# Attention with the value product turned round, logits as three products of split halves, and a ring of four heads

## What is computed

```python
logits = jnp.einsum('btkgd,btskd->btkgs', qg, k_sel).astype(f32) * ATT_SCALE
logits = jnp.where(valid[:, :, None, None, :], logits, -jnp.inf)
probs = jax.nn.softmax(logits, axis=-1).astype(v.dtype)
o = jnp.einsum('btkgs,btskd->btkgd', probs, v_sel)
return (o.reshape(B, L, ATT_WIDTH) * jax.nn.silu(z)) @ w_out
```

## Time and profile before

| | us |
|---|---|
| median of 3 runs | 1507.84 |
| lowest and highest | 1505.77, 1508.29 |
| the profiled execution | 1508.62 |
| its span | 1506.8 |
| busy in it: TensorE products, weight loads | 1404.7, 1220.5 |
| busy in it: VectorE, ScalarE, GpSimd | 933.7, 643.4, 559.2 |

### The profile page before, as it was taken

The page is one execution under the profiler, slowest core; times in us unless marked ns, Lnnn a source line. Parts: engine busy times, 40 slices in busy tenths (PEclk is TensorE's granted clock), DMA queues, the critical chain, the costliest instruction groups (busy, mean ns, idle before and its releaser), DMA issues. The chain is left out here.

```text
span 1506.8 us, 21428 instructions
## 1 busy us (share of the span) xinstructions
PE 1404.7 (93%) x8109; PEld 1220.5 (81%) x8109; DVE 933.7 (62%) x1765; ACT 643.4 (43%) x1136; POOL 559.2 (37%) x402
## 2 busy tenths in 40 slices
PE   4999999999996899999988999999999999998898
PEld 3999746999995455548878998989999999997786
DVE  7111388787793989744556676667676757576333
ACT  6233464677664555541122625243434343443121
POOL 4276501265553001100012646465555556464000
PEclk9999999999998999999998999999999999999899
DMA  6112100232312410001231101010101111105221
GB/s 223 29 43 57 28 1 15 72 87 75 96 48 67 140 29 15 4 24 63 100 88 43 43 20 57 20 57 20 57 27 50 35 43 34 43 6 201 99 85 63
DMA packets 96181, 86.79 MB, mean 58 GB/s; under 512 B 4528, under 2 KB 84272, under 8 KB 96080
## 3 DMA queue, kind: packets, MB, share of 16 engines
q1 hardware_dynamic: 94448, 80.60, 17.3%
q0 software_dynamic: 1632, 4.82, 0.9%
HBM read 65.43 MB, written 19.97 MB: 57 GB/s over the span
## 5 line engine op out<-in xcount | busy, mean ns | idle before, releaser
L186 PE MATMUL bank<-hn_hi,rw_hi 128*128 128x352 f32 x768 | 250.8, 327 | 1.5 <-PEq L1059 1.5
L186 PE MATMUL bank<-hn_hi,rw_lo 128*128 128x352 f32 x768 | 247.6, 322 | 0.0
L186 PE MATMUL bank<-hn_lo,rw_hi 128*128 128x352 f32 x768 | 247.3, 322 | 0.0
L186 PE MATMUL bank<-hn_hi,w_hi 128*128 128x352 f32 x672 | 218.9, 326 | 3.6 <-PEq L274 3.6
L186 PE MATMUL bank<-hn_lo,w_hi 128*128 128x352 f32 x672 | 216.4, 322 | 0.0
L186 PE MATMUL bank<-hn_hi,w_lo 128*128 128x352 f32 x672 | 216.2, 322 | 0.0
L186 PEld LDWEIGHTS bank<-hn_hi,rw_hi 128*128 128x128 f32 x768 | 144.9, 189 | 3.4 <-issue 3.0
L186 PEld LDWEIGHTS bank<-hn_lo,rw_hi 128*128 128x128 f32 x768 | 145.3, 189 | 0.0
L186 PEld LDWEIGHTS bank<-hn_hi,rw_lo 128*128 128x128 f32 x768 | 144.9, 189 | 0.0
L186 PEld LDWEIGHTS bank<-hn_hi,w_hi 128*128 128x128 f32 x672 | 126.9, 189 | 4.3 <-issue 3.7
L186 PEld LDWEIGHTS bank<-hn_lo,w_hi 128*128 128x128 f32 x672 | 127.2, 189 | 0.0
(11 more groups left out here) (233 smaller groups left out, 2950.5 us busy)
## 6 DMA issues: line engine op xcount, KB each, us to landing
rw_raw<-in_rec_w_in SPq DMA_DIRECT2D x32, 512.0 KB, 4.0
w_raw<-in_att_w_in SPq DMA_DIRECT2D x30, 512.0 KB, 4.0
q_rotated<-relu SPq DMA_DIRECT2D x24, 176.0 KB, 1.9
xin<-in_x_prompt SPq DMA_DIRECT2D x8, 512.0 KB, 4.1
q_tile<-q_rotated SPq DMA_DIRECT2D x8, 512.0 KB, 3.7
wo_raw<-in_att_w_out SPq DMA_DIRECT2D x4, 1024.0 KB, 10.0
x_again<-in_x_prompt SPq DMA_DIRECT2D x8, 512.0 KB, 4.1
residual<-h_rows SPq DMA_DIRECT2D x8, 512.0 KB, 2.9
```

The source lines that it names most:

```text
L186: last = pe.matmul(out, l, r, start=n == 0, stop=n == len(passes) - 1)
```

## The change

- **Value product.** It is made for each head. The transposed probabilities of a key tile are the loaded operand, and the 128 columns of a value head stream, so the output stands as queries by head width. It comes two items behind the transposes, at step i for item i-6. `pT` becomes a ring of four heads (`P_SLOTS`), freed head by head.
- **Sums.** The probabilities are no longer divided. Once for four heads VectorE takes the reciprocals (`divide`) and multiplies the output of the value product out of PSUM into `o_rows` (`scale`). TensorE turns each head back with a transpose into the same PSUM bank (`turn`), and the gate follows. The transposes of the probabilities wait for the exponential.
- **Logits** of tiles 2 to 7 (`FINE`): three float32r products of split halves in place of the plain one. ScalarE makes `kT_hi` at the block's start and `q_hi` of the next tile at head 4. VectorE makes `kT_lo` in the place of `kT`, keys 256 to 1023 at item 4 and the others at item 16, and `q_lo` of the next tile at head 5. Tiles 0, 1 and the sample keep the plain product.

```diff
+P_SLOTS = 4
...
-        S["pT"] = Space(nc, hi_at)("pT", [P, 2, 8, GROUP, P])
+        S["pT"] = Space(nc, hi_at)("pT", [P, P_SLOTS, 8, P])
+        S["kT_hi"] = Space(nc, hi_at + P_SLOTS * 8 * P * 4)("kT_hi", [P, KVH, SEQ], F32R)
+        S["q_hi"] = Space(nc, hi_at + (P_SLOTS + KVH) * 8 * P * 4)("q_hi", [P, 2, HEADS, P], F32R)
...
+        S["kT_lo"] = Space(nc, rest_at)("kT_lo", [P, KVH, T], F32R)
...
-    inv_done, probs_ready, pT_ready, pT_out = sem("inv_done"), sem("probs_ready"), sem("pT_ready"), sem("pT_out")
+    inv_done, scaled, turned, pT_ready, pT_out = sem("inv_done"), sem("o_scaled"), sem("o_turned"), sem("pT_ready"), sem("pT_out")
...
+    q_lo = Space(nc, space.at)("q_lo", [P, 2, HEADS, P], F32R)
...
+    q_hi, kT_hi, kT_lo = S["q_hi"], S["kT_hi"], S["kT_lo"]
+    k_hi_done, k_lo_done, q_hi_done, q_lo_done = sem("k_hi"), sem("k_lo"), sem("q_hi"), sem("q_lo")
+    FINE = range(2, SAMPLE)
+    o_rows = space("o_rows", [P, 2, GROUP, HD])
+    assert space.at <= S["third_at"]
...
         @block.sync
         def _(sp):
...
-                if h == 0:
-                    pe.wait_ge(q_in[t % 2], 16 * (t // 2 + 1))
-                src = kTs if t == SAMPLE else kT
+                if t in FINE:
+                    if h == 0:
+                        pe.wait_ge(k_lo_done, 2)
+                        pe.wait_ge(q_lo_done, t - 1)
+                    left, right = (x[:, t % 2, h, :] for x in (q_hi, q_lo)), (x[:, h // GROUP] for x in (kT_hi, kT_lo))
+                    (l_hi, l_lo), (r_hi, r_lo) = left, right
+                    passes = [(l_hi, r_hi), (l_hi, r_lo), (l_lo, r_hi)]
+                else:
+                    if h == 0:
+                        pe.wait_ge(q_in[t % 2], 16 * (t // 2 + 1))
+                    src = kTs if t == SAMPLE else kT
+                    passes = [(q[:, t % 2, h, 0:rows(t)], src[:, h // GROUP])]
...
-                    last = pe.matmul(logits[0:rows(t), i % 2, a:e], q[:, t % 2, h, 0:rows(t)],
-                                     src[:, h // GROUP, a:e], start=True, stop=True)
+                    for x, (l, r) in enumerate(passes):
+                        last = pe.matmul(logits[0:rows(t), i % 2, a:e], l, r[:, a:e], start=x == 0,
+                                         stop=x == len(passes) - 1)
...
             def transpose(i):
...
-                pe.wait_ge(probs_ready, i + 1)
+                pe.wait_ge(exp_done, i + 1)
...
-            def mix(g, quarter):
-                t, h = items[4 * g]
-                kv, r = h // GROUP, rows(t)
-                if quarter == 0:
-                    pe.wait_ge(pT_out, first_bank[4 * g + 4])
-                    if g >= 2:
-                        pe.wait_ge(gated, g - 1)
+            def mix(i):
+                t, h = items[i]
+                g, kv, r = i // GROUP, h // GROUP, rows(t)
+                pe.wait_ge(pT_out, first_bank[i + 1])
+                if g >= 2 and h % GROUP == 0:
+                    pe.wait_ge(gated, g - 1)
...
-                for j in range((n * quarter + 3) // 4, (n * (quarter + 1) + 3) // 4):
+                for j in range(n):
...
-                    last = pe.matmul(ps[2 + g % 2][:, 0:4 * r].rearrange("p (g q) -> p g q", g=4),
-                                     src[:, kv * HD:(kv + 1) * HD], pT[0:kr, g % 2, j, :, 0:r],
+                    last = pe.matmul(ps[2 + g % 2][0:r, (h % GROUP) * HD:(h % GROUP + 1) * HD],
+                                     pT[0:kr, i % P_SLOTS, j, 0:r], src[:, kv * HD:(kv + 1) * HD],
...
-                    if j == n - 1:
-                        last.then_inc(mixed, 1)
-            for i in range(N + LAG + 4):
+                last.then_inc(mixed, 1)
+            def turn(g):
+                r = rows(items[GROUP * g][0])
+                pe.wait_ge(scaled, g + 1)
+                for x in range(GROUP):
+                    last = pe.transpose(ps[2 + g % 2][:, x * r:(x + 1) * r], o_rows[0:r, g % 2, x, :], ident[0:r, 0:r])
+                last.then_inc(turned, 1)
+            for i in range(N + LAG + 5):
...
-                if i >= LAG + 4:
-                    mix((i - LAG - 4) // 4, (i - LAG) % 4)
+                if 0 <= i - LAG - 2 < N:
+                    mix(i - LAG - 2)
+                if i >= LAG + 7 and (i - LAG - 7) % GROUP == 0:
+                    turn((i - LAG - 7) // GROUP)
...
         @block.vector
         def _(dve):
...
-            def divide(i):
-                t, h = items[i]
-                r, n = rows(t), keys(t)
-                dve.wait_ge(exp_done, i + 1)
-                dve.reciprocal(low[0:r, 2, i:i + 1], low[0:r, 1, i:i + 1]).then_inc(inv_done, 1)
-                dve.wait_ge(inv_done, i + 1)
-                dve.tensor_scalar(probs[0:r, i % RING, 0:n], probs[0:r, i % RING, 0:n], low[0:r, 2, i:i + 1], None,
-                                  ALU.mult).then_inc(probs_ready, 1)
+            def divide(g):
+                r, of = rows(items[GROUP * g][0]), slice(GROUP * g, GROUP * (g + 1))
+                dve.wait_ge(exp_done, GROUP * (g + 1))
+                dve.reciprocal(low[0:r, 2, of], low[0:r, 1, of]).then_inc(inv_done, 1)
+            def scale(g):
+                r, of = rows(items[GROUP * g][0]), slice(GROUP * g, GROUP * (g + 1))
+                dve.wait_ge(inv_done, g + 1)
+                dve.wait_ge(mixed, GROUP * (g + 1))
+                dve.tensor_tensor(o_rows[0:r, g % 2], ps[2 + g % 2][0:r, :].rearrange("p (g d) -> p g d", g=GROUP),
+                                  low[0:r, 2, of].unsqueeze(2).to_broadcast([r, GROUP, HD]), ALU.mult).then_inc(scaled, 1)
...
             def gate(g):
...
-                dve.wait_ge(mixed, g + 1)
+                dve.wait_ge(turned, g + 1)
...
-            for i in range(N + 12):
+            def lower_keys(part):
+                of = (slice(2 * P, SEQ), slice(0, 2 * P))[part]
+                dve.tensor_tensor(kT_lo[:, :, of], kT[:, :, of], kT_hi[:, :, of].bitcast(F32),
+                                  ALU.subtract).then_inc(k_lo_done, 1)
+            def lower_queries(t):
+                dve.wait_ge(q_hi_done, t - 1)
+                dve.tensor_tensor(q_lo[:, t % 2], q[:, t % 2], q_hi[:, t % 2].bitcast(F32),
+                                  ALU.subtract).then_inc(q_lo_done, 1)
+            for i in range(N + 10):
+                if i == 4:
+                    dve.wait_ge(k_hi_done, 1)
+                    lower_keys(0)
+                if i == 2 * HEADS:
+                    lower_keys(1)
+                if i < N and items[i][1] == 5 and items[i][0] + 1 in FINE:
+                    lower_queries(items[i][0] + 1)
...
-                if 2 <= i <= N + 1:
-                    divide(i - 2)
-                if i >= 12 and i % 4 == 0:
-                    gate((i - 12) // 4)
+                if i >= 6 and i % 4 == 2 and i - 6 < N:
+                    divide((i - 6) // 4)
+                if i >= 10 and i % 4 == 2:
+                    scale((i - 10) // 4)
+                if i >= 13 and i % 4 == 1:
+                    gate((i - 13) // 4)
...
         @block.scalar
         def _(act):
+            def upper_queries(t):
+                act.wait_ge(q_in[t % 2], 16 * (t // 2 + 1))
+                if t >= 4:
+                    act.wait_ge(logits_ready, HEADS * (t - 1))
+                act.copy(q_hi[:, t % 2], q[:, t % 2]).then_inc(q_hi_done, 1)
+            act.copy(kT_hi[:], kT[:, :, 0:SEQ]).then_inc(k_hi_done, 1)
...
+                if i < N and items[i][1] == 4 and items[i][0] + 1 in FINE:
+                    upper_queries(items[i][0] + 1)
...
-                    g = (i - LAG) // 4
-                    if g >= 2 and h % 4 == 0:
-                        act.wait_ge(mixed, g - 1)
+                    if i - LAG >= P_SLOTS:
+                        act.wait_ge(mixed, i - LAG - P_SLOTS + 1)
...
-                        act.copy(pT[0:kr, g % 2, a:a + m, h % 4, 0:rows(t)],
+                        act.copy(pT[0:kr, (i - LAG) % P_SLOTS, a:a + m, 0:rows(t)],
...
```

## The result

The changed kernel took 1518.85 us (median of 4 runs, 1515.57 to 1520.6) against 1508.07 of the kernel before: ratio 1.007, 95% interval 1.0052 to 1.0089. It is slower by 0.7%, outside the forecast's range. On another chip the same kernel (e8_changed_again) came to 1.0061 (1.0038 to 1.0084). In the experiments the times of one kernel scatter by some 8 us to either side, and outside the attention block the profiled executions differ by up to 14 us (1313 to 1327) although nothing was edited there.

What follows compares the result with a forecast made beforehand. VectorE was taken to pace tiles 2 and 3, TensorE tile 5 onward, tile 4 nearly level. Stretch changes, mainly tile 6 -2.4 and tail +3.3, summed to -0.9 us: 1507.0 us, range 1504 to 1510 (1500 to 1514 with rivals).

Steps and rivals of the forecast that it cites:

- then idle of 0.3 to 0.6: Attention block stretches: each tile's time is TensorE's summed busy time plus only 0.3 to 0.6 us idle.
- two products of lead: Logits products running two heads ahead, counted as the argument against VectorE's order delaying TensorE.
- My sign of being wrong: Tiles 2 to 5 shortening by more than 1 us each, or TensorE waiting on L979 at heads 5 to 7.
- the rival that I gave 0.17: Head 5: query subtraction behind the scan, before logits subtraction, marking and gate, delays tiles 1 to 4; +7.3 us, chance 0.17.
- Tile 0: First stretch: VectorE's 1.8 us low-key subtraction at head 4, with TensorE's clock near its lower level, costs +1.0 us.
- TensorE's sums: TensorE busy time per stretch from logits, value product, turns: 13.2 us in tile 2 up to 31.0 in tile 7.
- The rates: TensorE issue spacing: 128-column split-half remainder 0.111 us; turned value product 0.114, range 0.111 to 0.118.
- the rival built on the rule: Serial loads: load and product not overlapping at 128 columns, 656 instructions at 0.10 us more, 1572 us; chance 0.03.
- The tail: Sample's last value products, transposes, turns, then last scaling, turn and gate: 11.5 us, +3.3.
- Tiles 6 and 7: Late stretches: tile 6 to take 28.7 us (-2.4), tile 7 31.5 us (-1.0).
- The stall: Tile 6: the 3.4 us VectorE stall on L989 moves to L964 at head 2, covered by two heads of lead.
- 29.8 forecast: VectorE's net relief in the block: division and most reciprocals removed, scalings and subtractions added; 29.8 us less.

Runs made afterwards that it cites:

- e6: The changed kernel with first key subtraction at item 0, gate at the head of its step, query subtraction at head 3 (conversion at head 2); ratio 0.9991.
- e1: The changed kernel with each group's gate at the head of its VectorE step, before the query and logits subtractions; ratio 1.0048.
- e5: The changed kernel with the first key subtraction at item 0 of VectorE's loop instead of item 4; block 200.59 us.
- e9: e6 with plain logits: no split halves, conversions or key and query subtractions; ratio 1.0046, block 197.46 us.
- e10: e6 with the sample tile's value product leaving out its last key tile of 32 rows, only to read the tail; tail 11.28 us.
- e7: e6 with the sample tile's old divided probabilities and four-head value product, plus an own buffer for the second group; ratio 0.996.
- e2: The changed kernel with the sample tile alone put back to divided probabilities and one value product for four heads; ratio 1.0036.
- e4: The changed kernel with the query subtractions and first key subtraction on GpSimd instead of VectorE; ratio 1.0079.

## Why the prediction was wrong

- **The step that failed** is the idle time of tiles 0 to 5, "then idle of 0.3 to 0.6", together with "two products of lead". TensorE was idle 3.5, 2.2, 1.2 and 1.3 us in tiles 2 to 5. The lead covers the logits, which is what I counted it for. The gate frees a PSUM bank, and that chain has less: the gate stood behind four VectorE instructions, from the scan on, and TensorE waited for it 7.9 us in tiles 1 to 3. My sign of being wrong was a wait on the logits subtraction instead.
- **That is the rival that I gave 0.17**, by its mechanism; its price was 7.3 us. e6 measures 9.9 for the whole of VectorE's order, or 8.4 against e8, at full clock in tile 2. The parts, by e8, e1 and e6 in turn: the gate's place gave 2.8 us in tiles 1 to 3 and took 1.5 in tiles 4 to 6; the keys in tile 0 gave 2.1; the query subtraction, moved beside that, gave 4.1 in tiles 2 to 6; tile 1, where the clock differs too, gave 0.9. So the query subtraction, which the rival priced, counts for more than the gate, which it only listed. No run moves it alone, and since the gate stood behind it in the same step, the two are not quite separate.
- **Tile 0** was mis-sized: +1.0 forecast, +2.4 measured. The subtraction held up TensorE at its lower clock: 7.33 us with it in the way, 5.14 without (e5).
- **TensorE's sums** were right, within 0.25 us in each of tiles 3 to 7, but partly by luck. By the busy times of e6 and e9 the split logits took 6.4 us off tiles 4 to 7 for 8.0 forecast; by e9 and the kernel before, the value product and its turns added 6.0 for 8.0. The two misses cancel. In tile 2 the sum was too high, 13.2 for 12.6 in e6. The rates were right: the remainder at 0.111, the value product at 0.112, the lower end of my range. By the rule of the Trainium skill, TensorE: Matmul & The Clock Gate, Part 3 (The mechanism), that a load overlaps only products of another row group, I had estimated 0.21; some 550 of the 576 instructions of tiles 0 to 7 stand 0.11 apart, so the trace disagrees, and the rival built on the rule is refuted here.
- **The tail** was mis-sized: 11.5 forecast, 13.7 measured. Seven sample heads cost 1.32 us each, not 1.11, which makes 1.5: the count of instructions was priced by a shape that never changes rows. By e10 about half of that comes with the 32-row tile; the other half is not explained. The turns took 0.9 us for 0.4 (673.36 to 673.94, 680.79 to 681.15), since tile 7's last turn falls into the tail. The last scaling, turn and gate took 1.6 us for the 1.7 I gave them (683.86, the end of the last product, to 685.46).
- **Tiles 6 and 7** came near the forecast, 29.0 and 31.1 for 28.7 and 31.5. The stall went where I put it: the marking step L992 (L964 before) took 7.0 us in 7 for 4.0, while L989 is gone.
- **VectorE** lost 24 us of busy time for 29.8 forecast; 3.0 of the difference is the stall that moved. Little came of it in tiles 0 to 5: they were bound by when the freeing instructions came, not by how much VectorE had to do.

The faster kernel e7 shows that the change's parts are sound. In a mended order the split logits give 3.9 us. The turned value product with plain logits (e9) takes 158.45 us in tiles 0 to 7 for 159.57 before. Only the 32-row tile loses by it.

## What to carry to other kernels

Before counting what an engine is relieved of, list for each ring and each PSUM bank which instruction frees it, and what stands ahead of that instruction in its engine's order; new work belongs in the lightest step, or where the engine waits anyway. A product turned round so that each head loads its own operand costs little at 128 columns, but multiplies the instructions of a tile with few rows: leave such a tile in the old form. In this kernel a wait of 2.5 us on TensorE could cost another 1.6 us in clock.

## What the runs showed of the hardware

- A split-half (float32r) product of 128 columns issues every 0.11 us, as each of the two instructions of a plain product of the same width does.
- In five profiled executions with the gate late (the changed kernel, e2, e4, e5, e8) TensorE waited 2.20 to 2.62 us for it at the end of tile 1 and 2.48 to 2.54 us in tile 2. Seven of these ten waits were followed by some 3.5 us at the lower clock, three were not, and the changed kernel shows both in tile 2 (17.10 and 15.51 us). The cause is open; the kernel before also had some 3.5 us at the lower clock in tile 1, with no wait over 0.7 us ahead of it in that tile.
- Beside GpSimd's subtraction of two SBUF tensors (2.57 us) a VectorE step with two SBUF inputs took 2.17 us for 0.61.
